# Twelve pairs of down-projection column blocks: the first four k tiles by seven block products (Strassen's algorithm)

## The chip, the cores and the metric

One core of a Trainium2 chip runs the whole kernel. The metric is the device time of one launch in microseconds (us). A TensorE matmul is called here by its moving width: one of 512 columns works on a stationary tile of 128x128 and a moving tile of 128x512.

## The reference, cut to what matters

```python
for layer in range(2):                      # x is (1, 256, 2048) float32
    h = rmsnorm(x, norm_mix_w[layer])
    x = x + mixer(h)                        # retention + RG-LRU, then windowed attention
    h = rmsnorm(x, norm_mlp_w[layer])
    u = relu(h @ w_up[layer])               # w_up   (2048, 8192)
    x = x + (u * u) @ w_down[layer]         # w_down (8192, 2048)
return rmsnorm(x, final_norm_w)
```

## The kernel before

**Blocks and steps.** All projections are cut into 89 blocks. A block is one product of the 256 tokens (two tiles of 128, `TT`) with a weight piece of 2048 rows (16 k tiles of 128) by 512 columns (`NB`), summed in two PSUM banks `acc[:, b % 2, tt]`. It is worked off in a *slot* of 8 *steps* (the code says halves), each of 2 k tiles (a half of one of four loaded *units* of 4 k tiles, 1 MB). float32 precision is had from three products of rounded parts: each operand is a high part and a low part, and a step issues, for 2 k tiles and 2 token tiles, high x high, high x low and low x high, so 12 matmuls of 512 columns (`products`, L1203 to L1218).

**The feeding of a step.** SyncE loads units into the four buffers `raw` (`load`, L488), each as soon as the low part of its last reader has been made. ScalarE rounds a step's 128x1024 weights to `w_hi` (`cut_hi`, L610), then VectorE forms `w_lo = raw - w_hi` (`cut_lo`, L848), and TensorE waits for that (L1207). `w_hi` and `w_lo` are rings of four steps (`RING`). Each engine runs a body once per step k of each slot: first `post(slot, k)`, which is the work on the block before, then the cut for step k + 4 (L811, L1165). The cut for step k + 4 waits until TensorE has used step k (L621). So a cut has three steps of TensorE's time to be finished in.

**The MLP.** An MLP is four chunks of 2048 hidden columns: a chunk is four "up" blocks, `up0` to `up3`, then four "down" blocks of the 2048x2048 piece of `w_down`. The loop of `run_slots` (L210) runs three chunks, a fourth stands behind it, and there are two MLPs.

**Post work of an up block**, in the slot behind it: ScalarE evacuates two token tiles with a ReLU and squares them (`leave`, L649, two times L672 and two times L677); VectorE turns them by 16 transposes of 32x256 (`turn_quadrants`, L1027, 4, 6 and 6 at steps 1, 2, 3); at step 4 ScalarE makes `b_hi` (L630) and VectorE `b_lo` (L862), two instructions each. For `up0` all this is two steps later (`late`, L125), since it is in `WOVEN`: its last two steps are run behind the first two of the block after it, so that a late stationary operand is not waited for. The first down block is woven in the same way.

**Post work of a down block**: VectorE adds its two PSUM banks to the residual `x` (L1070, two instructions of 128x512). TensorE starts block b only when block b - 2 has been evacuated (L1435 to L1440).

What the change touches: the sets and tables of L99 to L106, `late`, `quadrants_at`, `Slot.halves` (L199), the buffers of L284 to L315, `load`, `cut_hi` and `cut_lo`, ScalarE's and VectorE's `post` (L734, L1061), the adds of L1066 to L1070, `products`, and the `body` of each engine.

Of the kernel before, what the change touches and what calls it, by code (L numbers as in the profile page):

```python
# [28 lines left out]
P = 128  # L29
# [3 lines left out]
SEQ = 256  # L33
# [36 lines left out]
def mlp_blocks(last_kind):  # L70
    blocks = []
    for c in range(CHUNKS):
# [81 lines left out]

def quadrants_at(kind, b):

    return QUADRANTS_EARLY if b == ATT_OUT0 else QUADRANTS_AT[kind]


# [30 lines left out]
class Slot:  # L190
# [7 lines left out]

    def halves(self, n):  # L199

        return self.plus(self.b * HALVES + n, PERIOD * HALVES)

    def count(self, table, at, more=0):

# [46 lines left out]
def build(nc, t):  # L251
    ctx = ExitStack()
    with ctx:
# [30 lines left out]
        AREA = 12300  # L284
        area = sb("area", [P, AREA])
        place = {"at": 0}

# [15 lines left out]
        gate_t = take(LG, SEQ)  # L303
        q_t = take(HG, SEQ)
        k_t = take(HG, SEQ)
        v_tok = take(TT, NB)
        o_tok = take(TT, NB)
        p_ret = take(2, DECAY_W)
# [5 lines left out]
        gel = take(SEQ)  # L314
        gel2 = take(SEQ)  # L315
# [15 lines left out]
        den_s = take(TT, GROUP)  # L331
        den_i = take(TT, GROUP)
        final_w = take(D_MODEL)

        acc = ctx.enter_context(nc.psum_tensor("acc", [P, 2, TT, NB], F32))
        bank = ctx.enter_context(nc.psum_tensor("bank", [P, 4, NB], F32))
# [79 lines left out]
        y_act = sem("y_act")  # L416
        y_dve = sem("y_dve")
        stored = sem("stored")


        V_NORM = [0, KT, 2 * KT, 3 * KT]
# [15 lines left out]
        def stationary(b):  # L437

            from_b = (MIX_OUT0 <= b < MLP0 or ATT_OUT0 <= b < MLP1
                      or BLOCKS[b][0] == "down" or (b >= MLP0 and BLOCKS[b][0] in ("res", "fin")))  # L440
            return (b_hi, b_lo) if from_b else (a_hi, a_lo)

        def target(b):

# [11 lines left out]
        def _(sp):  # L456
# [30 lines left out]

            def load(slot, view):  # L488

                for q in range(UNITS):  # L490
                    b, k = piece(slot.b, 2 * q)

                    sp.wait_ge(lo_ready, slot.halves(2 * q + 2 - HALVES))
                    sp.dma_start(raw[:, q], view(row_groups(b)[k // 2], b - slot.b)).then_inc(raw_loaded[q], 16)

            def units(w):

# [111 lines left out]
        def _(act):  # L609
            def cut_hi(slot, n):  # L610

                d, h = divmod(n, HALVES)
                if slot.b * HALVES + n >= NBLK * HALVES:
                    return
                if slot.i is None and slot.b == 0 and d == 0:
                    act.wait_ge((raw_loaded if h % 2 else raw_first)[h // 2], 16)
                elif h % 2 == 0:
                    act.wait_ge(raw_loaded[h // 2], slot.plus(16 * (slot.b + d + 1), 16 * PERIOD))
                if slot.b * HALVES + n >= RING:

                    act.wait_ge(half_used, slot.halves(n - RING + 1))  # L621
                nc.scalar.activation(w_hi[:, h % RING], raw[:, h // 2, 2 * (h % 2):2 * (h % 2) + 2, :],  # L622
                                     ACT.Copy).then_inc(hi_ready, 1)

            def turned_parts(hi, kt, scale, n_turned, n_banks, by_quadrant=False):

# [84 lines left out]
            def attention(g, k):  # L711
# [16 lines left out]
                for tt in range(TT) if k == ATT_AT["out"] else ():  # L728
# [2 lines left out]
                                         bank[:, 2 - 2 * tt, :].rearrange("p (q s) -> p q s", q=PAIRS),  # L731
                                         ACT.Copy).then_inc(att_hi, 1)

            def post(slot, k):  # L734
                b = slot.b - 1
                if b < 0:
                    return
                kind, j = BLOCKS[b]
                if k == late(b) and kind in BY_ACT:
                    leave(slot, kind, j)  # L740
                if k == 1 + late(b) and kind in ("res", "fin"):
                    act.wait_ge(evac_dve, slot.count(N_EVAC_DVE, 0))
                    square_sums(next_norm(b), j)
                if kind in SPLIT and k == out_at(kind, b):
                    hi, _, kt, scale = target(b)
                    for m in range(2):
                        turned_parts(hi, kt + 2 * m, None if scale is None else scale + 2 * m,
                                     slot.count(N_MOVED, -1, INIT_HALVES + m + 1), m, kind in BY_QUADRANT)
                if k == 4 and kind == "res" and j == COLS - 1:
                    root(next_norm(b))  # L750
# [40 lines left out]
                    root(0)  # L791

            def body(slot):
                for k in range(HALVES):
# [44 lines left out]
        def _(dve):  # L839
# [7 lines left out]

            def cut_lo(slot, n):  # L848

                h = n % HALVES  # L850
                if slot.b * HALVES + n >= NBLK * HALVES:
                    return
                dve.wait_ge(hi_ready, slot.halves(n + 1))
                nc.vector.tensor_tensor(w_lo[:, h % RING], raw[:, h // 2, 2 * (h % 2):2 * (h % 2) + 2, :],  # L854
                                        w_hi[:, h % RING].bitcast(F32), ALU.subtract).then_inc(lo_ready, 1)

            def turned_parts(hi, lo, kt, scale, n_split, n_banks, by_quadrant=False):

# [202 lines left out]
            def post(slot, k):  # L1061
# [4 lines left out]
                if k == late(b) and kind in ("res", "down", "fin"):  # L1066
                    dve.wait_ge(half_used, slot.halves(late(b)))
                    for tt in range(TT):
                        xs = x[:, tt, j * NB:(j + 1) * NB]
                        nc.vector.tensor_tensor(xs, xs, acc[:, b % 2, tt, :], ALU.add).then_inc(evac_dve, 1)  # L1070
# [21 lines left out]
                if kind in TURNED and k == out_at(kind, b):  # L1092
                    for m in range(2):
# [4 lines left out]
                        elif kind in PLAIN:  # L1098
                            dve.wait_ge(turned, slot.count(N_MOVED, -1, INIT_HALVES + m + 1))
                            nc.vector.tensor_copy(plain_target(kind, j)(m),  # L1100
                                                  bank[:, m, :].rearrange("p (k s) -> p k s", k=2)
                                                  ).then_inc(turned_out, 1)
                if k == 3 + late(b) and kind == "fin" and j < COLS - 1:
                    weigh(j)
                if k == 3 and kind == "res" and j == COLS - 1:
# [39 lines left out]
                    inverse(0)  # L1145

            def body(slot):
                for k in range(HALVES):
# [53 lines left out]
        def _(pe):  # L1202
            def products(slot, k):  # L1203

                b, h = piece(slot.b, k)
                hi, lo = stationary(b)
                pe.wait_ge(lo_ready, slot.halves(k + 1))  # L1207
                for e in range(2):
                    kt = 4 * row_groups(b)[h // 2] + 2 * (h % 2) + e
                    wh, wl = w_hi[:, k % RING, e, :], w_lo[:, k % RING, e, :]  # L1210
                    first, last = h == 0 and e == 0, h == HALVES - 1 and e == 1
                    for tt in range(TT):
                        xh, xl = (s[:, kt, tt * P:(tt + 1) * P] for s in (hi, lo))
                        a = acc[:, b % 2, tt, :]
                        nc.tensor.matmul(a, xh, wh, start=first, stop=False)  # L1215
                        nc.tensor.matmul(a, xh, wl, start=False, stop=False)  # L1216
                        ins = nc.tensor.matmul(a, xl, wh, start=False, stop=last)  # L1217
                ins.then_inc(half_used, 1)  # L1218

            def turn_x(h):  # L1220
# [212 lines left out]
            def body(slot):  # L1433
# [9 lines left out]
                for k in range(HALVES):  # L1443
# [71 lines left out]
```

## Time and profile before

| | |
|---|---|
| median of three runs | 2006.84 us (2005.88 to 2007.82) |
| span of the profiled execution, first to last instruction | 2005.7 us |
| what lies around the span (median less span) | 1.1 us |
| busy share: TensorE matmul, weight load, VectorE, ScalarE | 100%, 82%, 72%, 51% |
| granted TensorE clock over the span | 1.00 (2.4 GHz) |
| DMA | 382 MB, 191 GB/s |

No device time of the profiled execution itself is given beside its span; the median of the runs stands in for it. The share of TensorE is of modelled durations (a matmul's record overlaps the next one's), so the rate is read from start to start. The other engines' times are averages over stages that differ much; what an edit in the down blocks costs is read from the rows of those slots.

### The profile page before, as it was taken

What the parts mean: (1) busy time and instruction counts of PE and PEld (TensorE: products, weight loads), DVE (VectorE), ACT (ScalarE), POOL (GpSimd) and SP (SyncE); (2) the same over time, 40 slices, a digit from 0 to 9 for tenths busy, and PEclk for the clock granted to TensorE, in tenths of its full rate; (3) what the DMA queues carried; (4) which work ended last, traced back from release to release, by engine and by line L of the source; (5) the groups of instructions that cost most, each with busy time, mean ns of one, the idle gap of its engine ahead of it and who ended that gap; (6) DMA issues with size and microseconds to landing.
All of it is one profiled execution on the core that took longest, in us unless ns stands there. A gap on an engine that the chain in (4) does not pass through costs nothing.

```text
span 2005.7 us, 24710 instructions
## 1 busy us (share of the span) xinstructions
PE 1997.1 (100%) x9161; PEld 1653.1 (82%) x9161; DVE 1450.5 (72%) x2028; ACT 1027.4 (51%) x1360; POOL 45.1 (2%) x55
## 2 busy tenths in 40 slices
PE   9999999999999999999999999999999999999998
PEld 8888888888888888888888878888888888888887
DVE  6777778987558647755889887988548756854875
ACT  6665665455345435434545566555435444534554
POOL 1110110000000000000000000000000000000000
PEclk9999999999999999999999999999999999999999
DMA  8556546556555565555655544565565555565563
GB/s 304 181 176 214 170 167 211 189 189 209 191 189 192 198 195 185 193 195 181 210 189 189 169 162 163 181 203 194 194 197 193 192 190 187 187 209 189 189 201 113
DMA packets 191756, 382.48 MB, mean 191 GB/s; under 512 B 6328, under 2 KB 7616, under 8 KB 191552
## 3 DMA queue, kind: packets, MB, share of 16 engines
q1 hardware_dynamic: 190288, 377.51, 57.0%
q0 software_dynamic: 1216, 3.88, 0.6%
q8 instruction: 48, 0.79, 0.2%
q14 instruction: 28, 0.23, 0.0%
q10 hardware_dynamic: 176, 0.07, 0.0%
HBM read 379.34 MB, written 2.10 MB: 190 GB/s over the span
## 4 chain that ended last, share of the span: by engine, by line
PE 98%; DVE 1%; issue 0%; ACT 0%; DMA 0%; ACTq 0%
PE acc L1215 31%; PE acc L1217 31%; PE acc L1216 31%; DVE area L1052 1%; PE bank L1305 0%; PE bank L1382 0%; PE bank L1406 0%; PE bank L1392 0%; DVE w_lo L854 0%; PE acc L1244 0%; PE acc L1248 0%; PE acc L1252 0%; PE bank L1347 0%; PE bank L1336 0%; PE bank L1337 0%
## 5 line engine op out<-in xcount | busy, mean ns | idle before, releaser
L854 DVE TENSOR_TENSOR w_lo<-raw,w_hi 128x1024 fp32r<-128x1024 f32 x708 | 858.9, 1223 | 497.8 <-ACT w_hi L622 494.9
L622 ACT ACTIVATE w_hi<-raw 128x1024 fp32r<-128x1024 f32 x708 | 743.5, 1060 | 772.3 <-PE acc L1217 771.0
L1215 PE MATMUL acc<-w_hi,a_hi 128*128 128x512 f32 x1552 | 607.1, 391 | 0.0
L1217 PE MATMUL acc<-w_hi,a_lo 128*128 128x512 f32 x1552 | 604.1, 389 | 0.0
L1216 PE MATMUL acc<-w_lo,a_hi 128*128 128x512 f32 x1552 | 604.0, 389 | 0.0
L1215 PE MATMUL acc<-w_hi,b_hi 128*128 128x512 f32 x1264 | 492.3, 389 | 0.0
L1216 PE MATMUL acc<-w_lo,b_hi 128*128 128x512 f32 x1264 | 491.8, 389 | 0.0
L1217 PE MATMUL acc<-w_hi,b_lo 128*128 128x512 f32 x1264 | 491.7, 389 | 0.0
L1215 PEld LDWEIGHTS acc<-w_hi,a_hi 128*128 128x128 f32 x1552 | 291.4, 188 | 61.2 <-issue 0.9
L1217 PEld LDWEIGHTS acc<-w_hi,a_lo 128*128 128x128 f32 x1552 | 291.3, 188 | 60.9
L1216 PEld LDWEIGHTS acc<-w_lo,a_hi 128*128 128x128 f32 x1552 | 291.4, 188 | 60.0
L1215 PEld LDWEIGHTS acc<-w_hi,b_hi 128*128 128x128 f32 x1264 | 237.2, 188 | 49.9 <-issue 0.9
L1217 PEld LDWEIGHTS acc<-w_hi,b_lo 128*128 128x128 f32 x1264 | 237.2, 188 | 49.4
L1216 PEld LDWEIGHTS acc<-w_lo,b_hi 128*128 128x128 f32 x1264 | 237.3, 188 | 49.2
L1052 DVE STREAM_TRANSPOSE turn<-stage 32x256 f32<-32x256 f32 x512 | 223.1, 436 | 7.7
L630 ACT ACTIVATE b_hi<-turn 128x512 fp32r<-128x512 f32 x64 | 37.0, 625 | 107.1 <-DVE turn L1052 107.1
L1052 DVE STREAM_TRANSPOSE turn<-x 32x256 f32<-32x256 f32 x192 | 83.7, 436 | 2.9
L672 ACT ACTIVATE stage<-acc,rinv 128x512 f32<-128x512 f32 x92 | 57.7, 675 | 0.5 <-DVE rinv L887 0.5
L1052 DVE STREAM_TRANSPOSE area<-stage 32x256 f32<-32x256 f32 x112 | 48.8, 436 | 1.6
L1070 DVE TENSOR_TENSOR x<-x,acc 128x512 f32<-128x512 f32 x78 | 49.8, 679 | 0.0
L862 DVE TENSOR_TENSOR b_lo<-turn,b_hi 128x512 fp32r<-128x512 f32 x64 | 41.1, 684 | 0.0
L677 ACT ACTIVATE stage<-stage 128x512 f32<-128x512 f32 x64 | 36.7, 626 | 0.0
(204 smaller groups left out, 602.1 us busy)
## 6 DMA issues: line engine op xcount, KB each, us to landing
raw<-in_mlp_w_up SPq DMA_DIRECT2D x128, 1024.0 KB, 5.3
raw<-in_mlp_w_down SPq DMA_DIRECT2D x128, 1024.0 KB, 5.1
raw<-in_hyb_w_in SPq DMA_DIRECT2D x44, 1024.0 KB, 5.2
raw<-in_attn_w_qkv SPq DMA_DIRECT2D x20, 1024.0 KB, 5.2
raw<-in_hyb_w_out SPq DMA_DIRECT2D x16, 1024.0 KB, 5.1
raw<-in_attn_w_out SPq DMA_DIRECT2D x16, 1024.0 KB, 5.0
raw<-in_hyb_w_in SPq DMA_DIRECT2D x5, 512.0 KB, 9.5
out_y<-x SPq DMA_DIRECT2D x4, 512.0 KB, 3.0
```

Of the source, the lines that this page charges most:

```text
L622: nc.scalar.activation(w_hi[:, h % RING], raw[:, h // 2, 2 * (h % 2):2 * (h % 2) + 2, :], ACT.Copy).then_inc(hi_ready, 1)
L630: nc.scalar.activation(hi[:, kt:kt + 2, :], src, ACT.Copy).then_inc(turned_hi, 1)
L672: ins = nc.scalar.activation(stage[:, tt, :], src, ACT.Relu if kind == "up" else ACT.Copy, scale=s)
L677: nc.scalar.activation(stage[:, tt, :], stage[:, tt, :], ACT.Square).then_inc(squared, 1)
L854: nc.vector.tensor_tensor(w_lo[:, h % RING], raw[:, h // 2, 2 * (h % 2):2 * (h % 2) + 2, :], w_hi[:, h % RING].bitcast(F32), ALU.subtract) ...
L862: nc.vector.tensor_tensor(lo[:, kt:kt + 2, :], src, hi[:, kt:kt + 2, :].bitcast(F32), ALU.subtract).then_inc(turned_out, 1)
L1052: ins = nc.vector.transpose(dst[f * QUAD:(f + 1) * QUAD, :, :, a, :], src[a * QUAD:(a + 1) * QUAD, :, :, f, :])
L1070: nc.vector.tensor_tensor(xs, xs, acc[:, b % 2, tt, :], ALU.add).then_inc(evac_dve, 1)
L1215: nc.tensor.matmul(a, xh, wh, start=first, stop=False)
L1216: nc.tensor.matmul(a, xh, wl, start=False, stop=False)
L1217: ins = nc.tensor.matmul(a, xl, wh, start=False, stop=last)
```

## The change

For 12 pairs of neighbouring down blocks (the four of chunks 0, 1 and 2 in each MLP) the first four k tiles are computed by Strassen's algorithm in Winograd's form: the operands are seen as 2x2 blocks (token tile x k-tile pair, and k-tile pair x column block), and seven products of 6 matmuls take the place of eight. The slot of the pair's first block holds 18 steps, one of them empty, and that of the second holds 2. Steps ("P", p) are the seven products; ("L", h) and ("R", h) are ordinary steps of the left and the right block for h of 2 to 7. The right block is summed in `acc`, the left one in two banks of `bank`.

What is new in a pair: VectorE forms four sums of weights in place in `raw`, 128x1024 each (`add_weights`, behind the cuts of SUM_AFTER), and adds four partial results from PSUM to `x`, 128x512 each (`add_part`, at the step behind P1, P5, P6 and P7). TensorE waits for the first of these before P6, the second before P3, the third before P7. Once in a chunk, behind the turning of `up0`, VectorE forms four token sums of 128x256 (`add_tokens`), ScalarE their high parts and VectorE their low parts, 128x1024 each.

```diff
+QUADRANTS_PAIR = {8: 5, 9: 5, 10: 6}
+PAIR_CHUNKS = CHUNKS - 1
+PAIRS0 = {m + PERIOD * c + COLS + 2 * n for m in (MLP0, MLP1) for c in range(PAIR_CHUNKS) for n in range(2)}
+PAIR_STEPS = [("P", 1), ("L", 2), ("P", 5), ("L", 3), ("P", 6), ("P", 2), ("P", 4), ("P", 7), ("P", 3),
+              ("L", 4), ("L", 5), ("R", 2), ("R", 3), ("R", 4), ("R", 5), ("R", 6), ("R", 7), (None, 0),
+              ("L", 6), ("L", 7)]
+PAIR_SPLIT = 18
+PAIR_FREE = [STEP_OF["P", 4] + 1, STEP_OF["P", 3] + 1, STEP_OF["L", 3] + 1, STEP_OF["L", 5] + 1,
+             STEP_OF["R", 3] + 1, STEP_OF["R", 5] + 1, STEP_OF["R", 7] + 1, STEP_OF["L", 7] + 1]
+SUM_AFTER = {STEP_OF["P", 1]: 5, STEP_OF["P", 5]: 6, STEP_OF["L", 3]: 7, STEP_OF["P", 2]: 4}
+SUM_COUNT = {5: 1, 6: 2, 7: 3, 4: 4}
 WOVEN = ({MIX_OUT0, QKV0, ATT_OUT0}
-         | {m + COLS * n for m in (MLP0, MLP1) for n in range(2 * CHUNKS)})
+         | {m + COLS * n for m in (MLP0, MLP1) for n in range(2 * CHUNKS)}) - PAIRS0
@@ def late(b)
+    if b + 1 in FIRST_PAIRS:
+        return 1
@@ ScalarE, cut_hi
+                elif what is not None and what[0] == "P" and what[1] in SUM_COUNT:
+                    act.wait_ge(weights_added, slot.pairs(4, SUM_COUNT[what[1]], b))
@@ VectorE, cut_lo
+                if b in PAIRS0 and h in SUM_AFTER:
+                    add_weights(slot, b, SUM_AFTER[h])
+            def add_weights(slot, b, p):
+                b11, b21, b12, b22 = (raw[:, q, 2 * e:2 * e + 2, :] for q in range(2) for e in range(2))
+                if p == 5:
+                    ins = nc.vector.tensor_tensor(b11, b12, b11, ALU.subtract)
+                if p == 6:
+                    ins = nc.vector.tensor_tensor(b11, b22, b11, ALU.subtract)
+                if p == 7:
+                    ins = nc.vector.tensor_tensor(b12, b22, b12, ALU.subtract)
+                if p == 4:
+                    ins = nc.vector.tensor_tensor(b21, b21, b11, ALU.subtract)
+                ins.then_inc(weights_added, 1)
+            def add_part(slot, k):
+                for p, tt, cols, src in ((1, 0, left, 1), (5, 1, right, 0), (6, 0, right, 1), (7, 1, left, 1)):
+                    if k == STEP_OF["P", p] + 1:
+                        dve.wait_ge(half_used, slot.halves(k))
+                        nc.vector.tensor_tensor(x[:, tt, cols], x[:, tt, cols], accumulator(slot.b, src),
+                                                ALU.add).then_inc(part_added, 1)
+            def add_tokens(slot):
+                nc.vector.tensor_tensor(s1, a21, a22, ALU.add).then_inc(tokens_added, 1)
+                nc.vector.tensor_tensor(s3, a11, a21, ALU.subtract).then_inc(tokens_added, 1)
+                dve.wait_ge(tokens_added, slot.chunks(4, 1))
+                nc.vector.tensor_tensor(s2, s1, a11, ALU.subtract).then_inc(tokens_added, 1)
+                dve.wait_ge(tokens_added, slot.chunks(4, 3))
+                nc.vector.tensor_tensor(s4, a12, s2, ALU.subtract).then_inc(tokens_added, 1)
@@ VectorE, post
+                if slot.b in PAIRS0:
+                    add_part(slot, k)
+                if b + COLS in FIRST_PAIRS and k == out_at(kind, b):
+                    add_tokens(slot)
+                if b + COLS in FIRST_PAIRS and k == HALVES - 1:
+                    tokens_rest(slot)
@@ TensorE
+            def product(slot, k, p):
+                pe.wait_ge(lo_ready, slot.halves(k + 1))
+                if p in (3, 6, 7):
+                    pe.wait_ge(part_added, slot.pairs(4, {6: 1, 3: 2, 7: 3}[p]))
...
+                for e in range(2):
...
+                    nc.tensor.matmul(a, xh, wh, start=first, stop=False, skip_group_check=True)
+                    nc.tensor.matmul(a, xh, wl, start=False, stop=False, skip_group_check=True)
+                    ins = nc.tensor.matmul(a, xl, wh, start=False, stop=False, skip_group_check=True)
+                ins.then_inc(half_used, 1)
```

Not shown: the counts of steps per slot that the semaphore values follow, the order in which `load` fetches the pair's eight units, a wait before ("R", 6) for `up3`'s turned tokens, and buffers of the mixer that now share space (`v_tok` with `o_tok`, `gel` and `gel2` with `junk`), which make room for the token sums.

## Rows read from the trace of the kernel before

**Rows 1.** The page: span, and busy time by engine.
```profile
span 2005.7 us, 24710 instructions
...
PE 1997.1 (100%) x9161; PEld 1653.1 (82%) x9161; DVE 1450.5 (72%) x2028; ACT 1027.4 (51%) x1360; POOL 45.1 (2%) x55
```

**Rows 2.** The page: the chain that ended last, by engine.
```profile
PE 98%; DVE 1%; issue 0%; ACT 0%; DMA 0%; ACTq 0%
```

**Rows 3.** Timeline, PE: first matmul of the slots behind up1 and up3.
```profile
429.33 0.39 PE L1215 MATMUL acc<-w_hi,a_hi 128*128 128x512 f32 x1
...
472.85 0.39 PE L1215 MATMUL acc<-w_hi,b_hi 128*128 128x512 f32 x1
```

**Rows 4.** Stretches: us, busy of PE, PEld, DVE, ACT, POOL; clock; DMA.
```profile
0.00:5.00 5.00, 3.29 (x14) 2.99 (x15) 0.55 (x2) 1.49 (x2) 0.31 (x5) 1.00 0.55 178
...
463.00:485.00 22.00, 22.00 (x99) 18.22 (x98) 17.96 (x27) 11.74 (x15) 0.00 (x0) 1.00 0.57 195
485.00:507.00 22.00, 22.00 (x99) 18.22 (x98) 15.26 (x20) 9.42 (x10) 0.00 (x0) 1.00 0.61 206
```

**Rows 5.** Groups of instructions, shapes apart: busy us, mean ns of one, idle before.
```profile
L854 DVE TENSOR_TENSOR w_lo<-raw,w_hi 128x1024 fp32r<-128x1024 f32 x708 | 858.9, 1223 | 497.8 <-ACT w_hi L622 494.9
L622 ACT ACTIVATE w_hi<-raw 128x1024 fp32r<-128x1024 f32 x708 | 743.5, 1060 | 772.3 <-PE acc L1217 771.0
...
L1070 DVE TENSOR_TENSOR x<-x,acc 128x512 f32<-128x512 f32 x78 | 49.8, 679 | 0.0
...
L866 DVE SCALAR_TENSOR_TENSOR a_lo<-turn,vecs,a_hi 128x256 fp32r<-128x256 f32 x48 | 20.0, 478 | 0.0
...
L1023 DVE TENSOR_TENSOR area<-area 128x1024 f32<-128x1024 f32 x8 | 9.8, 1224 | 0.3
```

**Rows 6.** Timeline, DVE: start, us, idle before; the slots of up2, up3, downs.
```profile
430.66 2.35 DVE L854 TENSOR_TENSOR w_lo<-raw,w_hi 128x1024 fp32r<-128x1024 f32 x2
434.53 1.23 DVE L854 TENSOR_TENSOR w_lo<-raw,w_hi 128x1024 fp32r<-128x1024 f32 x1 [1.53 <-ACT w_hi L622]
...
445.39 1.22 DVE L854 TENSOR_TENSOR w_lo<-raw,w_hi 128x1024 fp32r<-128x1024 f32 x1
...
468.74 2.35 DVE L854 TENSOR_TENSOR w_lo<-raw,w_hi 128x1024 fp32r<-128x1024 f32 x2
471.43 1.23 DVE L854 TENSOR_TENSOR w_lo<-raw,w_hi 128x1024 fp32r<-128x1024 f32 x1 [0.34 <-ACT w_hi L622]
474.14 1.23 DVE L854 TENSOR_TENSOR w_lo<-raw,w_hi 128x1024 fp32r<-128x1024 f32 x1 [1.49 <-ACT w_hi L622]
...
502.49 1.27 DVE L1070 TENSOR_TENSOR x<-x,acc 128x512 f32<-128x512 f32 x2
```

**Rows 7.** Timeline, ACT: the same stretches.
```profile
429.37 1.99 ACT L622 ACTIVATE w_hi<-raw 128x1024 fp32r<-128x1024 f32 x2
431.27 1.25 ACT L672 ACTIVATE stage<-acc,rinv 128x512 f32<-128x512 f32 x2
...
433.45 1.05 ACT L622 ACTIVATE w_hi<-raw 128x1024 fp32r<-128x1024 f32 x1
...
473.05 1.06 ACT L622 ACTIVATE w_hi<-raw 128x1024 fp32r<-128x1024 f32 x1 [1.66 <-PE acc L1217]
...
476.20 1.06 ACT L622 ACTIVATE w_hi<-raw 128x1024 fp32r<-128x1024 f32 x1
```

**Rows 8.** Timeline, all engines: TensorE released by a late VectorE result.
```profile
1136.31 0.48 DVE L995 MEMSET bank<- 64x512 f32 x1
...
1136.85 0.48 PEld L1382 LDWEIGHTS bank<-area 64*64 64x64 f32 x21 [0.58 <-DVE bank L995]
```

**Rows 9.** Timeline, PE: first two matmuls behind a break in the stream.
```profile
25.45 0.48 PE L1215 MATMUL acc<-w_hi,a_hi 128*128 128x512 f32 x1
...
25.76 0.40 PE L1216 MATMUL acc<-w_lo,a_hi 128*128 128x512 f32 x1
```

**Rows 10.** DMA issues: count, KB each, median us from issue to landing.
```profile
raw<-in_mlp_w_down SPq DMA_DIRECT2D x128, 1024.0 KB, 5.1
```

More of the change, by code:

```diff
@@ new lines, with ring, step_at, pair_step @@
+NSTEP = [PAIR_SPLIT if b in PAIRS0 else len(PAIR_STEPS) - PAIR_SPLIT if b in PAIRS1 else HALVES
+         for b in range(NBLK)]
+STEP0 = [sum(NSTEP[:b]) for b in range(NBLK + 1)]
+def ring(b, k):
+    return (STEP0[b] + k) % RING
+def step_at(b, n):
+    while b < NBLK and n >= NSTEP[b]:
+        n -= NSTEP[b]
+        b += 1
+    return b, n
+def pair_step(b, k):
+    if b in PAIRS0:
+        return PAIR_STEPS[k]
+    if b in PAIRS1:
+        return PAIR_STEPS[PAIR_SPLIT + k]
+    return None
@@ L107, with weight_at @@
+def weight_at(b, k):
+    what = pair_step(b, k)
+    if what is None:
+        return k // 2, k % 2, b + 1
+    side, h = what
+    first = b if b in PAIRS0 else b - 1
+    if side == "P":
+        q, e = PIECE_OF[h]
+        return q, e, first + 1
+    n = PAIR_UNITS.index((side, h // 2))
+    return n % UNITS, h % 2, first + 1 + n // UNITS
 WOVEN_ORDER = ([(0, k) for k in range(6)] + [(1, 0), (1, 1), (0, 6), (0, 7)]
@@ L199, in halves, with pairs, chunks @@
     def halves(self, n):
-        return self.plus(self.b * HALVES + n, PERIOD * HALVES)
+        per = STEP0[self.b + PERIOD] - STEP0[self.b] if self.i is not None else 0
+        return self.plus(STEP0[self.b] + n, per)
+    def pairs(self, per, n, b=None):
+        return self.plus(per * sum(p < (self.b if b is None else b) for p in PAIRS0) + n, 2 * per)
+    def chunks(self, per, n):
+        return self.plus(per * sum(p + 1 < self.b for p in FIRST_PAIRS) + n, per)
     def count(self, table, at, more=0):
@@ L732, in attention, with tokens @@
                                          ACT.Copy).then_inc(att_hi, 1)
+            def tokens(slot):
+                act.wait_ge(tokens_added, slot.chunks(4, 4))
+                nc.scalar.activation(s_hi[:, :, :, :], s_sum[:, :, :, :], ACT.Copy).then_inc(tokens_hi, 1)
             def post(slot, k):
@@ L793, in body @@
             def body(slot):
-                for k in range(HALVES):
+                for k in range(NSTEP[slot.b]):
                     post(slot, k)
@@ L848, in cut_lo @@
             def cut_lo(slot, n):
-                h = n % HALVES
-                if slot.b * HALVES + n >= NBLK * HALVES:
+                b, h = step_at(slot.b, n)
+                if b >= NBLK:
                     return
+                what = pair_step(b, h)
+                if what == (None, 0):
+                    return
+                q, e, _ = weight_at(b, h)
                 dve.wait_ge(hi_ready, slot.halves(n + 1))
-                nc.vector.tensor_tensor(w_lo[:, h % RING], raw[:, h // 2, 2 * (h % 2):2 * (h % 2) + 2, :],
-                                        w_hi[:, h % RING].bitcast(F32), ALU.subtract).then_inc(lo_ready, 1)
+                nc.vector.tensor_tensor(w_lo[:, ring(b, h)], raw[:, q, 2 * e:2 * e + 2, :],
+                                        w_hi[:, ring(b, h)].bitcast(F32),
+                                        ALU.subtract).then_inc(lo_ready, 2 if what == ("R", HALVES - 1) else 1)
@@ new lines, in add_part @@
+            def add_part(slot, k):
+                left, right = (slice((BLOCKS[slot.b + d][1]) * NB, (BLOCKS[slot.b + d][1] + 1) * NB) for d in (0, 1))
+                for p, tt, cols, src in ((1, 0, left, 1), (5, 1, right, 0), (6, 0, right, 1), (7, 1, left, 1)):
[3 more added lines that the diff above has]
+                                                ALU.add).then_inc(part_added, 1)
@@ L857, in turned_parts, with tokens_rest @@
+            def tokens_rest(slot):
+                dve.wait_ge(tokens_hi, slot.chunks(1, 1))
+                nc.vector.tensor_tensor(s_lo[:, :, :, :], s_sum[:, :, :, :], s_hi[:, :, :, :].bitcast(F32),
+                                        ALU.subtract).then_inc(tokens_lo, 1)
             def turned_parts(hi, lo, kt, scale, n_split, n_banks, by_quadrant=False):
@@ L1068, in post @@
                     for tt in range(TT):
-                        xs = x[:, tt, j * NB:(j + 1) * NB]
-                        nc.vector.tensor_tensor(xs, xs, acc[:, b % 2, tt, :], ALU.add).then_inc(evac_dve, 1)
+                        c = BLOCKS[b + (b in PAIRS0) - (b in PAIRS1)][1]
+                        xs = x[:, tt, c * NB:(c + 1) * NB]
+                        nc.vector.tensor_tensor(xs, xs, accumulator(b, tt), ALU.add).then_inc(evac_dve, 1)
                 if k == 1 + late(b):
@@ L1147, in body @@
             def body(slot):
-                for k in range(HALVES):
+                for k in range(NSTEP[slot.b]):
                     post(slot, k)
@@ L1203, in products @@
             def products(slot, k):
-                b, h = piece(slot.b, k)
+                what = pair_step(slot.b, k)
+                if what is None:
+                    b, h = piece(slot.b, k)
+                    begins = h == 0
+                else:
+                    side, h = what
+                    b = slot.b + (side == "L") - (slot.b in PAIRS1)
+                    begins = what == PAIR_STEPS[1]
+                joins = what is not None
                 hi, lo = stationary(b)
@@ L1209, in products @@
                     kt = 4 * row_groups(b)[h // 2] + 2 * (h % 2) + e
-                    wh, wl = w_hi[:, k % RING, e, :], w_lo[:, k % RING, e, :]
-                    first, last = h == 0 and e == 0, h == HALVES - 1 and e == 1
+                    wh, wl = w_hi[:, ring(slot.b, k), e, :], w_lo[:, ring(slot.b, k), e, :]
+                    first, last = begins and e == 0, h == HALVES - 1 and e == 1
                     for tt in range(TT):
                         xh, xl = (s[:, kt, tt * P:(tt + 1) * P] for s in (hi, lo))
[L1214 to L1217, printed above, removed]
+                        a = accumulator(b, tt)
+                        nc.tensor.matmul(a, xh, wh, start=first, stop=False, skip_group_check=joins)
+                        nc.tensor.matmul(a, xh, wl, start=False, stop=False, skip_group_check=joins)
+                        ins = nc.tensor.matmul(a, xl, wh, start=False, stop=last, skip_group_check=joins)
@@ new lines, in products @@
+                ins.then_inc(half_used, 2 if what == ("R", HALVES - 1) else 1)
+            def product(slot, k, p):
+                b = slot.b
+                pe.wait_ge(lo_ready, slot.halves(k + 1))
+                if p == 5 and b in FIRST_PAIRS:
+                    pe.wait_ge(tokens_lo, slot.chunks(1, 1))
+                if p in (3, 6, 7):
+                    pe.wait_ge(part_added, slot.pairs(4, {6: 1, 3: 2, 7: 3}[p]))
+                a = accumulator(b, 1 if p in (1, 6, 7) else 0)
+                if p in (2, 4):
+                    a = accumulator(b + 1, p // 2 - 1)
+                for e in range(2):
+                    wh, wl = w_hi[:, ring(b, k), e, :], w_lo[:, ring(b, k), e, :]
+                    if p in (1, 2, 4):
+                        kt, tt = {1: (e, 0), 2: (2 + e, 0), 4: (2 + e, 1)}[p]
+                        xh, xl = (s[:, kt, tt * P:(tt + 1) * P] for s in (b_hi, b_lo))
+                    else:
+                        xh, xl = (s[:, {5: 0, 6: 1, 7: 2, 3: 3}[p], e, :] for s in (s_hi, s_lo))
+                    first = p in (1, 5) and e == 0
+                    nc.tensor.matmul(a, xh, wh, start=first, stop=False, skip_group_check=True)
+                    nc.tensor.matmul(a, xh, wl, start=False, stop=False, skip_group_check=True)
+                    ins = nc.tensor.matmul(a, xl, wh, start=False, stop=False, skip_group_check=True)
@@ L1442, in body @@
                     pe.wait_ge(turned_out, slot.count(N_TURNED, -1, INIT_HALVES))
-                for k in range(HALVES):
+                for k in range(NSTEP[b]):
+                    what = pair_step(b, k)
+                    if what == (None, 0):
+                        continue
+                    if what is not None and what[0] == "P":
+                        product(slot, k, what[1])
+                        continue
+                    if b in FIRST_PAIRS and k == LAST_TURNED_AT:
+                        pe.wait_ge(turned_out, slot.count(N_TURNED, 0, INIT_HALVES))
+                    if what == ("R", 2):
+                        pe.wait_ge(part_added, slot.pairs(4, 4))
                     if b == 0 and k >= PIECED:
```

76 lines of the change are left out of this document (60 added, 16 removed).

## The prediction
> **What bounds the kernel now.** I read the page first: the span is 2005.7 us and TensorE is busy for all of it, VectorE for 72%, ScalarE for 51% [rows 1]. The chain that ended last is 98% TensorE [rows 2]. So TensorE's stream of matmuls is the bound, and what the others do is free while they stay ahead of it. The pace: two slots of 96 matmuls lie between the two starts in [rows 3], 43.52 us, which is 0.2267 us for a matmul, 2.72 for a step of 12 and 1.36 for a product of 6. The clock is 1.00 throughout [rows 4], so nothing is to be won there.
>
> The share of 72% hides where VectorE is near its limit. Over the post work of up blocks it is busy 17.96 of 22 us, in the stretch behind, mostly down steps, 15.26 [rows 4]. Each step needs one cut by ScalarE (1.06 us) and one by VectorE (1.22) [rows 5], in that order, and a cut may begin only when the step four before has been used. From that step's end it is 0.20 to ScalarE's start and 1.09 more to VectorE's [rows 3, 7, 6] (472.85, 473.05, 474.14), so a cut is ready 2.5 us behind, with 8.16 allowed: VectorE can run 5.6 us late before TensorE feels it. In the seven products the same three steps last only 4.08, and the reserve falls to 1.5.
>
> **What it removes.** One product of 6 matmuls in each of 12 pairs: 72 x 0.2267 = 16.3 us, all on the path, if TensorE never waits.
>
> **What it adds, by pair.** Seven cuts serve the first k tiles instead of four: three more on ScalarE (1.06) and VectorE (1.22). Four weight sums on VectorE: fp32 tensor_tensor of 128x1024 from SBUF, for which the attention's own row has 1.224 us [rows 5]. Four part adds of 0.68 [rows 5]. That is 3.7 + 4.9 + 2.7 = 11.3 us more VectorE work in 40 us of TensorE's, which the average could hold. But it is crowded: all of it belongs to the first 15 us of a pair or shortly before. So I walk the queue in the program's order. Back to back, VectorE's instructions follow each other faster than they last: a cut after 1.12 (two in 2.35), a part add after 0.59 (two in 1.27) [rows 6]; I take 1.14 for a cut and a weight sum, 0.60 for an add, and full durations where another engine waits. A TensorE step held by VectorE starts some 0.14 behind: 0.06 to the release (1136.79 to 1136.85 [rows 8]) and 0.08 for the longer first interval (0.31 for 0.23 [rows 9]).
>
> **Second pair of a chunk.** Time 0 is the start of ("L", 6) of the pair before, which frees the ring for the cut of P1. VectorE's starts: P1 1.30, sum for P5 2.44, L2 3.58, two evacuations of the right block 4.72 (end 5.99), P5 5.91, sum for P6 7.05, L3 8.19, sum for P7 9.33, two evacuations of the left block 10.47, P6 11.67, add of P1 12.81 (end 13.50), P2 13.41, sum for P4 14.55 (end 15.78). Now ScalarE must round that sum, 15.82 to 16.88, before VectorE can go on: P4 16.92 (end 18.15), add of P5 18.06, P7 18.66, P3 19.80, add of P6 20.94, end 21.63. TensorE: P1 may not overwrite `acc` before the evacuation, so it starts at 6.13 instead of 5.44 (0.69 late); L2, P5, L3, P6, P2 follow without a gap to 17.02; P4 waits for its low part until 18.29 (1.27); P7 waits for the add of P6, since it accumulates on what that add reads, from 19.65 to 21.77 (2.12). Sum 4.1 us.
>
> The add of P6 decides because it stands in VectorE's queue behind the cuts of P7 and P3, which are ahead of their use. Thirteen cuts and sums, seven adds and evacuations are 19.0 us, from 1.30 on; P7 is due at 17.7. Even without the 1.2 us in which VectorE waits for ScalarE, it would be 2.8 late. Behind it only cuts at ordinary pace follow, and the queue recovers.
>
> **First pair.** Time 0 is its start, like 472.85 in [rows 3]. VectorE's cut of P1 starts at -4.11 (468.74 [rows 6], late because of up2's turning), then sum -2.97, L2 -1.83, P5 -0.60, sum 0.54, L3 1.68, sum 2.82, P6 3.96, add of P1 5.10. ScalarE rounds P6 at 1.81 and then evacuates and squares up3, so the cut of P2 starts 3.15 later (473.05 to 476.20 [rows 7]), 4.96; VectorE has it at 6.06, sum 7.20, ScalarE P4 8.47, VectorE P4 9.57 (end 10.80), add of P5 10.71, P7 11.31, P3 12.45, add of P6 13.59, end 14.28. TensorE wants P4 at 10.88 and gets it at 10.94, wants P7 at 12.30 and gets it at 14.42. Sum 2.2 us. Up3's turning comes five to seven steps later, at steps of 2.72, and by the same walk its `b_lo` is done 1.1 us before ("R", 6) asks: nothing.
>
> **Token sums, once a chunk.** They stand behind up0's `b_lo`, before the cut that starts at 430.66 [rows 6]. Four adds of 128x256: the nearest row is 0.478 us [rows 5]; with two waits on own results some 1.7. Then ScalarE's part (1.06) and VectorE's (1.14). ScalarE's evacuation of up1 (431.27 [rows 7]) waits in its queue behind these: the token part starts at 432.47, the cut behind it at 433.44, the evacuation at 434.41, 3.1 us later than before. Up1's turning and the cuts between move with it: the cut that started at 445.39 [rows 6] starts at 448.5 and ends at 449.8, while its step is due at 429.33 + 7 x 2.72 = 448.4 [rows 3]. Stall 1.5 us. If the adds took 0.2 each it would be under 0.6; if ScalarE's gap were filled, nothing. At up3's slot the queue has caught up.
>
> **Costed at nothing.** The loads: a unit lands 5.1 us after its issue [rows 10]. The tightest is the first right unit, issued when P4's low part is made (18.15), landed at 23.3, when ScalarE's queue comes to it (P7 is used at 23.1); its step is due 8.2 us after P7's start. If it came 3 us late it would still be hidden. The lost weaving: the down steps that need up3 now come at step 15. The shared mixer buffers: no wait is added and their readers are in order; bounded by 0 and 1 us.
>
> **Sum.** Per chunk 1.5 + 2.2 + 4.1 = 7.8 us, six chunks 47.0; less 16.3 is +30.7 on a span of 2005.7, so 2036.4, and with the 1.1 us between span and median of the runs **2037.5 us**.
>
> [...]
>
> **The rivals.**
> 1. *VectorE stalls TensorE as walked* (2024 to 2056): 0.78. Low end: no stall at the token sums (-9) and the waits of VectorE on ScalarE half as long (-5). High end: 0.1 us more for each cut and sum between unlike instructions, 13 in either walk and some 6 in the token stretch, +19.
> 2. *VectorE keeps up* (faster). What speaks for it: the stretch over down blocks has 6.7 us idle of 22 [rows 4]. It needs the add of P6 to end within 17.7 us of ("L", 6), so its queue from 1.30 on must shrink from 20.3 to 16.2, which weight sums of some 0.2 us instead of 1.14 would do in the second pair. Then 16.3 are won: 1990.5. Against it, the sum has the same shape, type and operation as the row of 1.224. 0.07. If stalls just eat the gain (2.7 us a chunk), about 2007: 0.05.
> 3. *More than walked*: the first right unit and those queued behind it land late, or sums in place cost more than between two buffers. Five us more a chunk is 2067: 0.06.
> 4. *The clock falls.* In the first 5 us TensorE was busy for 3.29 and the granted clock was 1.00 [rows 4]; in the walk it is busy for about as much of the 5 us around a stall of 2.1. Were the steps from P1 to P3 of each pair, 15 us, at 1.2 GHz, 12 x 15 = 180 more would give about 2217: 0.04. The Trainium skill ("TensorE: Matmul & The Clock Gate", section "HAM oscillation") warns that gaps in the matmul stream throw TensorE back to 1.2 GHz; the row shows no fall at such a share.
>
> **How the numbers follow.** 0.2% (4 us) is about what a measurement of this kernel can tell from no change. Faster 0.07, same 0.05, slower 0.88. The range 2024 to 2056 is case 1's own and leaves out the others.
>
> **What would show it.** In the profile after: TensorE's busy share below 100%, with waits of TensorE for the part add and for `w_lo` of some 40 us together; 72 matmuls fewer; chunks with P7 about 2.1 us late in either pair, P4 1.3 late in the second pair only, P1 0.7 late in the second only; one stall of 1.5 us near the end of up1's post work; VectorE without idle from the second pair's P1 cut to P6's add, but for about 1.2 us. Wrong would be: no waits of TensorE (case 2), waits for DMA (case 3), a granted clock under 1.00 (case 4), or a weight sum that is not 1.2 us.

## The result, and the profile after

The changed kernel takes 2048.21 us (median of four runs, 2044.73 to 2050.33) against 2007.07 us (four runs; the 2006.84 given before are three of them): the ratio is 1.0206, with a 95% interval of 1.0192 to 1.0221. It is slower by 41 us, where 30.7 were forecast; 2048.2 lies inside the range of 2024 to 2056.

The page of the changed kernel, its span, busy shares and the chain that ended last (compare [rows 1, 2]):

```profile
span 2048.5 us, 25055 instructions
...
PE 2004.6 (98%) x9089; PEld 1644.6 (80%) x9089; DVE 1584.1 (77%) x2190; ACT 1067.0 (52%) x1402; POOL 45.2 (2%) x55
...
PE 71%; DVE 16%; issue 8%; ACT 5%; ACTq 0%; DMA 0%; DVEq 0%
```

The profiled execution of the changed kernel is the slowest of its four (2050.33 us). The 72 matmuls are gone (9161 to 9089). The chain, 98% TensorE before, now runs through VectorE for 16% and ScalarE for 5%, though VectorE's share of the span rose only from 72 to 77%. The share says little; the chain says who is late.

The weight loads' waits (engine, line waited for: us in total, times, longest) say where. L1420 is the first matmul of a product, L1000 the part add, L974 the low part of a cut:

```profile
PEld acc L1420 <- DVE x L1000: 26.9, 12, 2.2
PEld acc L1394 <- DVE w_lo L974: 9.9, 14, 1.4
PEld bank L1420 <- DVE w_lo L974: 8.5, 12, 1.2
PEld acc L1420 <- issue: 5.6, 6, 0.9
```

In the order of the rows: P7, held in every pair for the part add of P6; the step in the slot of up1's post work, twice in each of six chunks (two short waits of 0.3 together lie elsewhere); P4, where the longest are the six of the second pairs (the first pairs have 0.23 each); P1 of the second pairs. The last row names no releaser; the matmul's own row names the evacuation, L1235:

```profile
PE acc L1420 <- DVE x L1235: 3.1, 6, 0.5
```

Together the four rows are 50.9 us, where the prediction named some 40. Behind each wait the first interval between matmuls is some 0.1 longer, and the ordinary gap between weight loads (about 0.04) is contained in the rows.

One second pair in VectorE's timeline (start, us, idle before). The walk's time 0 lies at 513.5:

```profile
520.53 1.22 DVE L987 TENSOR_TENSOR raw<-raw 128x1024 f32<-128x1024 f32 x1
521.67 1.22 DVE L974 TENSOR_TENSOR w_lo<-raw,w_hi 128x1024 fp32r<-128x1024 f32 x1
...
528.00 1.22 DVE L991 TENSOR_TENSOR raw<-raw 128x1024 f32<-128x1024 f32 x1
530.43 1.23 DVE L974 TENSOR_TENSOR w_lo<-raw,w_hi 128x1024 fp32r<-128x1024 f32 x1 [1.21 <-ACT w_hi L731]
531.57 0.68 DVE L1000 TENSOR_TENSOR x<-x,acc 128x512 f32<-128x512 f32 x1
532.17 2.35 DVE L974 TENSOR_TENSOR w_lo<-raw,w_hi 128x1024 fp32r<-128x1024 f32 x2
534.44 0.68 DVE L1000 TENSOR_TENSOR x<-x,acc 128x512 f32<-128x512 f32 x1
```

The sum for P6 was walked at 7.05 and stands at 7.0; the add of P6 was walked at 20.94 and stands at 20.9. The sum for P4 ends at 529.2, ScalarE rounds it, VectorE idles 1.21 us, then come the cut of P4, the add of P5, the cuts of P7 and P3, and only then the add for which TensorE waits. TensorE's timeline of the same pair:

```profile
530.57 0.39 PE L1422 MATMUL bank<-w_hi,b_lo 128*128 128x512 f32 x1
531.71 0.50 PE L1420 MATMUL bank<-w_hi,b_hi 128*128 128x512 f32 x1 [0.75 <-DVE w_lo L974]
532.04 0.39 PE L1421 MATMUL bank<-w_lo,b_hi 128*128 128x512 f32 x1
...
532.97 0.40 PE L1422 MATMUL bank<-w_hi,b_lo 128*128 128x512 f32 x1
535.17 0.50 PE L1420 MATMUL acc<-w_hi,s_hi 128*128 128x512 f32 x1 [1.81 <-DVE x L1000]
535.52 0.40 PE L1421 MATMUL acc<-w_lo,s_hi 128*128 128x512 f32 x1
...
536.87 0.63 PE L1420 MATMUL acc<-w_hi,s_hi 128*128 128x512 f32 x1
537.30 0.63 PE L1421 MATMUL acc<-w_lo,s_hi 128*128 128x512 f32 x1
```

P4 comes 1.14 behind its predecessor instead of 0.23, P7 2.20. The last two rows show what was not in the sum of the forecast: from 536.4 on, eight matmuls follow each other at 0.43 instead of 0.23. Two stretches of the same pair, and the one around P7 of the first pair that had a fall too (us, busy of PE, PEld, DVE, ACT, POOL; clock; DMA):

```profile
531.10:536.20 5.10, 2.68 (x10) 1.91 (x11) 5.10 (x7) 3.20 (x4) 0.00 (x0) 1.00 0.59 204
536.50:539.50 3.00, 3.00 (x9) 2.33 (x8) 2.19 (x3) 1.06 (x1) 0.00 (x0) 0.50 1.00 375
...
1421.82:1426.92 5.10, 3.28 (x14) 2.22 (x13) 5.10 (x7) 3.20 (x4) 0.00 (x0) 1.00 0.60 204
```

In the second pair TensorE was busy for 2.68 of 5.10 us, and right behind it the granted clock is 0.50, the level of 1.2 GHz. The stretch lasts 3.41 us and costs 1.7. The trace has seven of them while TensorE has work, in all six second pairs and one first pair, always beginning 1.2 to 1.4 us behind P7's late start.

**The account.** One weight sum as the chain of waits has it in two chunks that follow each other (start us, us, what):

```profile
652.29 1.23 DVE raw L985
...
833.21 1.23 DVE raw L985
```

With one such stretch in between, that is 180.9 us for a chunk, where eight slots of 21.76 were 174.1 [rows 3]. Of the 6.8 more, 1.7 are the clock. The other 5.1 are 7.85 of lost time less 2.7 for the removed matmuls. The intervals between matmuls show what the 7.85 are made of: about 7.3 at the places where TensorE was held, and the rest intervals that are slightly longer than 0.2267 without a wait. Over six chunks and seven stretches: 6 x 5.1 + 7 x 1.7 = 42.7, and the spans differ by 42.8.

### The profile page after: what moved, and what is told of

The parts are those of the page before. It is cut to its first block, busy times and chain, and to the rows that moved or that the text cites. A ratio compares the mean times of both kernels' runs of the same rounds, so it can differ in the third digit from the quotient of the medians.

```text
span 2048.5 us, 25055 instructions
## 1 busy us (share of the span) xinstructions
PE 2004.6 (98%) x9089; PEld 1644.6 (80%) x9089; DVE 1584.1 (77%) x2190; ACT 1067.0 (52%) x1402; POOL 45.2 (2%) x55
## 4 chain that ended last, share of the span: by engine, by line
PE 71%; DVE 16%; issue 8%; ACT 5%; ACTq 0%; DMA 0%; DVEq 0%
PE acc L1394 20%; PE acc L1395 20%; PE acc L1396 20%; DVE w_lo L974 5%; DVE turn L1216 5%; ACT w_hi L731 3%; PE bank L1394 2%; PE bank L1395 2%; PE bank L1396 2%; DVE x L1000 1%; ACT stage L781 1%; PE acc L1420 1%; PE acc L1422 1%; DVE raw L987 1%; DVE raw L985 1%
## 5 line engine op out<-in xcount | busy, mean ns | idle before, releaser
L974 DVE TENSOR_TENSOR w_lo<-raw,w_hi 128x1024 fp32r<-128x1024 f32 x744 | 901.0, 1223 | 406.6 <-ACT w_hi L731 403.3
L1394 PE MATMUL acc<-w_hi,b_hi 128*128 128x512 f32 x784 | 305.6, 390 | 0.0
L1395 PE MATMUL acc<-w_lo,b_hi 128*128 128x512 f32 x784 | 305.1, 389 | 0.0
L1396 PE MATMUL acc<-w_hi,b_lo 128*128 128x512 f32 x784 | 305.0, 389 | 0.0
L1394 PEld LDWEIGHTS acc<-w_hi,b_hi 128*128 128x128 f32 x784 | 147.2, 188 | 31.5 <-issue 0.9
L1396 PEld LDWEIGHTS acc<-w_hi,b_lo 128*128 128x128 f32 x784 | 147.2, 188 | 30.7
L1395 PEld LDWEIGHTS acc<-w_lo,b_hi 128*128 128x128 f32 x784 | 147.2, 188 | 30.2
L1394 PE MATMUL bank<-w_hi,b_hi 128*128 128x512 f32 x288 | 113.7, 395 | 0.0
L1395 PE MATMUL bank<-w_lo,b_hi 128*128 128x512 f32 x288 | 112.5, 391 | 0.0
L1396 PE MATMUL bank<-w_hi,b_lo 128*128 128x512 f32 x288 | 112.3, 390 | 0.0
L1394 PEld LDWEIGHTS bank<-w_hi,b_hi 128*128 128x128 f32 x288 | 55.0, 191 | 12.1
```

Of the source, the lines that this page charges most:

```text
L974: nc.vector.tensor_tensor(w_lo[:, ring(b, h)], raw[:, q, 2 * e:2 * e + 2, :], w_hi[:, ring(b, h)].bitcast(F32), ALU.subtract).then_inc(lo_ ...
L1394: nc.tensor.matmul(a, xh, wh, start=first, stop=False, skip_group_check=joins)
L1395: nc.tensor.matmul(a, xh, wl, start=False, stop=False, skip_group_check=joins)
L1396: ins = nc.tensor.matmul(a, xl, wh, start=False, stop=last, skip_group_check=joins)
```

## The experiments

All times are medians beside runs of the kernel before on the same chip, whose median was 2005.7 to 2005.9 us there. The changed kernel was not run again beside them; its 2048.21 stands beside 2007.07, so a difference taken from it is uncertain by some 1 us.

**p6_early.** One add moved by one place.

```diff
-                    if k == STEP_OF["P", p] + 1:
-                        dve.wait_ge(half_used, slot.halves(k))
+                    if k == STEP_OF["P", p] + (p != 6):
+                        dve.wait_ge(half_used, slot.halves(STEP_OF["P", p] + 1))
```

> VectorE's part add of P6 is moved one place up its queue, ahead of the weight cut of P3. Theory 1 (VectorE's queue holds TensorE): the add ends 1.14 us earlier in either pair, so each of the 12 waits before P7 falls from about 2.1 to 1.0 us and the time falls by 13.7 us, from 2048.2 to 2034.5; should the clock then no longer fall to 1.2 GHz, by the 12 us of the seven falls as well, to 2022.5. Theory 2 (the products themselves or their PSUM traffic are slow, and the waits only mark the place): nothing that VectorE does in another order helps, 2048 within 4.

Measured: 2024.12 us, ratio 1.0092 (1.0075 to 1.0109), and the clock was not at 0.50 in either MLP. The waits of P7:

```profile
PEld acc L1420 <- DVE x L1000: 13.3, 12, 1.1
PEld acc L1394 <- DVE w_lo L974: 9.8, 14, 1.4
PEld bank L1420 <- DVE w_lo L974: 8.5, 12, 1.2
```

26.9 became 13.3: 13.6 us less, where the walk says 13.7, and the other rows stand still. The remaining 10.5 of the 24.1 us won are put down to the clock: the seven stretches, 11.9 us in the trace of the changed kernel, are gone. So the place of one instruction of 0.68 us in VectorE's queue was worth 24 us of 2048. Theory 2 falls.

**tokens_later.** The parts of the token sums in up2's slot.

```diff
-                if b + COLS in FIRST_PAIRS and k == HALVES - 1:
+                if b + COLS - 1 in FIRST_PAIRS and k == HALVES - 2:
                     tokens(slot)
...
+                if b + COLS - 1 in FIRST_PAIRS and k == 0:
+                    dve.wait_ge(tokens_added, slot.chunks(4, 4))
-                if b + COLS in FIRST_PAIRS and k == HALVES - 1:
+                if b + COLS - 1 in FIRST_PAIRS and k == HALVES - 2:
                     tokens_rest(slot)
```

> The high and low parts of the token sums are made in up2's slot instead of up1's; the four adds stay. Theory 1: ScalarE's evacuation of up1 moves back by only 1.7 us instead of 3.1, the cut that missed its step by 1.4 now ends on time, and the stalls of 0.2 and 1.4 us in that slot go: 8 to 9 us less, about 2039.5. The clock falls, which all stand in the pairs, stay. Theory 2 (the stall there is of the adds alone): under 2 us, 2047.

Measured: 2044.72 us (2041.35 to 2048.3), 3.5 less than the changed kernel and not the 8.7 expected. In the trace the stall is gone whole: of the 9.9 us in which a step waited for `w_lo` in `acc` the two short ones elsewhere, 0.3 in all, are left, the other two are unchanged (26.9 and 8.5), and the profiled execution, with eight stretches of half clock, has a span of 2039.6, which is 8.9 less, or 10.6 at equal clock. Some 9 of the 10.6 lie in the six chunks, 1.5 in each (from P7 of one first pair to the next, 181.1 us with two stretches where the changed kernel has 180.9 with one). The mean granted clock of the four runs was 0.989 to 0.992, where those of the changed kernel had 0.993 to 0.995: more stretches at half clock, in a number that differs from run to run, ate the rest of the gain. By an estimate from these means, at 1.7 us a stretch and with the end of the span, at half clock in both, taken off, the changed kernel had 5 to 7 and this one 8 to 12. The mechanism is as walked; the expectation that the clock's falls would stay the same was wrong.

**no_sums.** `SUM_AFTER` and `SUM_COUNT` empty.

> The four sums of weights are left out (the products then read the plain weights, so this part of the computation is wrong), and ScalarE's waits for them; cuts, part adds and token sums stay. Theory 1: VectorE's queue is 4.6 us shorter and never waits for ScalarE in it; by the same walk only 0.55 us before each P7 is left of 6.2 us per chunk, the clock no longer falls, and with the token stall (1.4) the time is about 2005.7 - 16.3 + 6 x 2.5 + 2 + 1.5 = 2008. Theory 2 (part adds and the extra cuts alone are too much, or the products are slow): above 2030.

Measured: 2006.96 us (2006.52 to 2008.24 in ten runs), ratio 1.0005 (0.9995 to 1.0014), no fall of the clock.

```profile
PEld acc L1394 <- DVE w_lo L974: 10.5, 16, 1.4
PEld acc L1420 <- DVE x L1000: 8.1, 12, 0.7
```

P7 still comes late in each pair: it starts 0.64 behind its predecessor instead of 0.23, and the next interval is 0.1 longer, 0.5 in all where the walk has 0.55. P4 and P1 are on time. So the four sums, with ScalarE's waits for them, 12 x 4 x 1.22 = 59 us of VectorE's work, cost 41 us of the kernel's time, the clock's 12 among them; what is left just eats the removed matmuls. Theory 1 holds.

**evac_early.** The evacuation ahead of the cut of L2.

```diff
+                if slot.b in PAIRS0 and k == PAIR_SPLIT - 1:
+                    dve.wait_ge(half_used, slot.halves(PAIR_SPLIT))
+                    for tt in range(TT):
...
+                        nc.vector.tensor_tensor(xs, xs, accumulator(slot.b, tt), ALU.add).then_inc(evac_dve, 1)
-                if k == late(b) and kind in ("res", "down", "fin"):
+                if k == late(b) and kind in ("res", "down", "fin") and b not in PAIRS0:
```

> VectorE evacuates the right block one place earlier, ahead of the cut of L2. Theory 1: P1 of the second pair is no longer held (0.7 us), but VectorE's queue is as long as before, so P4 waits 1.9 instead of 1.3 and P7 the same 2.1: time unchanged, 2048 within 2 (or the clock's falls vary by one or two, 1.7 us each). Theory 2 (each wait is a cost of its own): 6 x 0.7 = 4 us less, 2044.

Measured: 2048.63 us against 2048.21.

```profile
PEld acc L1426 <- DVE x L1000: 26.9, 12, 2.2
PEld bank L1426 <- DVE w_lo L974: 13.4, 12, 2.0
PEld acc L1400 <- DVE w_lo L974: 9.7, 14, 1.4
```

P1's wait is gone, P4's grew from 8.5 to 13.4. The time is unchanged, as theory 1 has it. Here a wait taken away in front of a full queue came back at the next place: the length of VectorE's queue up to the add of P6 decides, not the single waits.

**three_edits.** p6_early, tokens_later and evac_early together, order of the steps unchanged.

> The order of the steps as in the changed kernel, with P6's add ahead of the cut of P3, the token parts in up2's slot and the right block's evacuation ahead of the cut of L2. Theory 1: 3.75 us of waiting per chunk by the walk (P4 1.9 and P7 1.0 in the second pair, P7 0.8 in the first), 2005.7 - 16.3 + 22.5 + 2.5 = 2014.4, so that spreading the products is worth the other 20 us. Theory 2 (moving the adds only moves the waits): 2020 or more.

Measured: 2016.74 us, ratio 1.0054 (1.0038 to 1.0069); no fall of the clock, though P4 of the second pair came 1.97 us behind its predecessor and P7 1.06. That is 2.3 more than theory 1 has, and below the 2020 of theory 2.

**spread_only.** A third ordinary step of the left block, L4, is put between the products (L2 and L3 stood there already), P7 is moved ahead of P4, and the loads follow the order in which buffers come free. Not shown: the table of the buffers' release (`PAIR_FREE`) that follows from it, and one step more of waiting for the first two units of an MLP.

```diff
-PAIR_STEPS = [("P", 1), ("L", 2), ("P", 5), ("L", 3), ("P", 6), ("P", 2), ("P", 4), ("P", 7), ("P", 3),
-              ("L", 4), ("L", 5), ("R", 2), ("R", 3), ("R", 4), ("R", 5), ("R", 6), ("R", 7), (None, 0),
+PAIR_STEPS = [("P", 1), ("L", 2), ("P", 5), ("L", 3), ("P", 6), ("L", 4), ("P", 2), ("P", 7), ("P", 4), ("P", 3), ("L", 5),
+              ("R", 2), ("R", 3), ("R", 4), ("R", 5), ("R", 6), ("R", 7), (None, 0),
-PAIR_UNITS = [("L", 0), ("R", 0), ("L", 1), ("L", 2), ("R", 1), ("R", 2), ("R", 3), ("L", 3)]
+PAIR_UNITS = [("L", 0), ("R", 0), ("L", 1), ("L", 2), ("R", 2), ("R", 3), ("R", 1), ("L", 3)]
...
-                for q in range(UNITS):
+                for q in (2, 0, 1, 3) if b0 in PAIRS1 else range(UNITS):
```

> Only the order of the steps and of the loads is changed; P6's add, the token parts and the evacuation stay as in the changed kernel. Theory 1: by the walk 0.7 us before P1 and 0.8 before P7 of the second pair are left, with the 1.4 us of the token sums 2.9 per chunk, no clock falls: 2005.7 - 16.3 + 17.4 + 2.5 = 2009.3. Theory 2: as the changed kernel less the clock's 12 us, 2036.

Measured: 2018.34 us, ratio 1.0060 (1.0045 to 1.0076), no fall of the clock. 30 us less than the changed kernel, but 9 more than expected. TensorE's and ScalarE's timelines at P1 of a second pair show where most of the 9 lie:

```profile
514.57 0.39 PE L1398 MATMUL bank<-w_hi,b_lo 128*128 128x512 f32 x1
516.57 0.49 PE L1422 MATMUL acc<-w_hi,b_hi 128*128 128x512 f32 x1 [1.61 <-DVE x L1237]
```

```profile
512.93 3.13 ACT L733 ACTIVATE w_hi<-raw 128x1024 fp32r<-128x1024 f32 x3 [2.31 <-DMA raw<-in_mlp_w_down]
```

The new places of the units let a load of the next pair start later, ScalarE waited 2.31 us for it, and VectorE's queue and the evacuation behind it moved along: P1 came 2.00 behind its predecessor instead of 0.90 (1.88 to 2.04 in the six chunks), some 6.4 us in all. The walk had no loads in it. P7 of the second pair came only 0.59 behind its predecessor, so less was lost there than walked; the rest of the 9 was not traced.

**all_four.** spread_only and three_edits together.

> The seven products are spread among ordinary steps (P1 L2 P5 L3 P6 L4 P2 P7 P4 P3 L5, with the loads in the order that their buffers come free), P6's part add stands ahead of the next cut, the token parts are made in up2's slot, and the right block is evacuated ahead of the cut of L2. Theory 1: VectorE's work per pair is the same to an instruction, but it is due over five more microseconds; the walk leaves 0.35 us of waiting per chunk, no clock falls, and the 72 matmuls are won but for some 2.5 us of longer intervals in the products: 2005.7 - 16.3 + 2.1 + 2.5 = 1994. Theory 2 (VectorE is simply too full in the chunk, 11 us more work per pair): waits turn up elsewhere, at the ordinary steps, and the time stays above 2010.

Measured: 1997.07 us, ratio 0.9954 (0.9940 to 0.9967). Faster than the kernel before, by 0.46%. The walk had 1994, 3 us less; theory 2 falls. The page has TensorE's share at 100% again:

```profile
span 1993.5 us, 25061 instructions
...
PE 1984.2 (100%) x9089; PEld 1636.3 (82%) x9089; DVE 1582.6 (79%) x2190; ACT 1068.3 (54%) x1402; POOL 45.1 (2%) x55
```

Of the weight loads' waits for a part add this is left:

```profile
PEld acc L1430 <- DVE x L1002: 2.5, 7, 0.6
```

VectorE's work is what it was in the changed kernel (1584.1 us there); its due times and its order differ. Neither half was enough alone: spread_only has 2018.34 and three_edits 2016.74.

**all_four_again.** The same kernel, run beside the one below.

> The same kernel as all_four, beside loads_first on the same chip: 1997 within 1.5 by either theory.

Measured: 1997.23 us, ratio 0.9953 (0.9940 to 0.9967).

**loads_first.** all_four, with the early free buffer also loaded first in a second pair.

```diff
-                for q in (2, 0, 1, 3) if b0 in PAIRS1 else range(UNITS):
+                for q in (2, 0, 1, 3) if b0 in PAIRS1 or b0 - 1 in PAIRS1 and b0 in PAIRS0 else range(UNITS):
```

> As all_four, but for a second pair the left block's second unit, whose buffer comes free first, is also issued first. In all_four ScalarE's cut for P1 and L2 of the second pair waited for that load (it landed 7.8 us after its issue), 0.3 us before P1 in VectorE's queue, and TensorE lost 0.8 us per chunk. Theory 1: the wait for DMA goes, P1 and P6 of the second pair start on time or 0.3 earlier, and 1 to 3 us are won: about 1995 where all_four has 1997. Theory 2 (the 0.8 us are VectorE's own queue): no difference.

Measured: 1995.09 us (1994.69 to 1996.0), ratio 0.9945 (0.9931 to 0.9958), beside all_four at 1997.23 (1995.49 to 1997.46). ScalarE's waits for the down weights fell from 36.9 us (20 times, all_four) and 33.1 (18 times, all_four_again) to 19.1 (12 times):

```profile
ACT w_hi L733 <- DMA raw<-in_mlp_w_down: 19.1, 12, 2.4
```

This is the best kernel of the study, 0.55% under the one before. The profiled executions of both have practically the same span (1993.8 and 1993.5), so of the 2 us only the medians speak, and the intervals of the two ratios overlap: that TensorE gains by it is not shown. ScalarE's waits for the weight sum of P5 (L987) grew at the same time from 10.5 to 19.9 us.

## Why the prediction was right, and where it was off

- *The matmuls removed*: 72, as counted. In the trace of the changed kernel the intervals inside the second pair's crowded stretch are 0.2311 us on average (46 intervals from 519.94 to 530.57) where 0.2267 was taken; in no_sums the same 46 intervals are 0.2302, so it is not the weight sums that make them longer. Over the chunks with pairs such intervals add up to some 3.7 us, not in the forecast, and not traced further.
- *Second pair, 4.1 us*: P1 0.67, P4 0.91, P7 1.97 late by the intervals (0.90, 1.14, 2.20 less 0.23), with 0.10 to 0.12 more behind each, 3.9 in all. P4 was walked 1.27 and took 1.0; TensorE had itself lost 0.2 by the longer intervals before it.
- *First pair, 2.2 us*: P4 0.1 and P7 2.1, as walked. "Up3's turning: nothing" held.
- *Token sums, 1.5 us*: 1.3 by the intervals, 1.5 by what tokens_later won in a chunk, by way of ScalarE's evacuation as walked; tokens_later took it away.
- *VectorE decides by its queue up to the add of P6*: shown by p6_early (13.6 us of waiting gone for one place in the queue) and evac_early (nothing won).
- *A weight sum of 1.22 us*: 1.219 to 1.222 in four groups of 12, and the next instruction 1.13 to 1.14 behind it (520.53 to 521.67 above), as taken in the walk.
- *What failed* is the step "the clock falls", put as a rival at 0.04 and at nothing in the sum. The argument was that at 3.29 us busy of 5 the clock had stayed at 1.00 [rows 4] and that a stall of 2.1 leaves about as much. Around P7 of the second pair the busy time was 2.68 of 5.10, lower than that row, since P4's and P7's stalls lie 3.5 us apart and add up; but first pairs had a fall too, one in this trace, at 3.28 of 5.10, and four in that of tokens_later. So a row from the first microseconds was no bound for a gap of 2.2 us in the stream. The price was off as well: not 15 us a pair, but one stretch of 3.41 us at half clock, 1.7 us, in seven of twelve pairs: 11.9 us. With that the forecast of +30.7 on the span becomes +42.6, and 42.8 was measured. The rest of the sum, 7.8 us per chunk, came out at 7.85. That closeness is in part luck: the waits themselves are 0.5 shorter than walked, and the slightly longer intervals, which the sum did not have, make up for it. The term was mis-sized, at 0 instead of 12; the mechanism that was forecast carried the other 31.
- *The other rivals*: VectorE all but kept up only where the sums were left out, or the products spread and the queues reordered (2007 and 1997). Loads did not hold TensorE in the changed kernel, though ScalarE waited 12.9 us for down weights (51.4 in p6_early, where TensorE's other waits stood still); they did once the products were spread.

## What to carry to other kernels

Saved matmuls count only if the engines that feed TensorE can prepare the replacement in the time it is due, so walk their queues in program order at the crowded place; shares over the span (72 to 77% here) show nothing of it. When a wait names an instruction, look at what stands ahead of that instruction on its engine: moving one add of 0.68 us past one cut won 24 us, and spreading the short products, together with three changes of the order in the queues, turned a loss of 41 us into a gain of 9. Price a stall with what it does to the clock as well: here gaps of 2.2 us between two matmuls cost up to 1.7 us beyond their length, and gaps of 2.04 and less did not.

## What the runs showed of the hardware that was not expected

Every stretch at 1.2 GHz in the MLPs came behind a gap in which two matmuls started 2.20 to 2.22 us apart, and none came in the profiled executions whose gaps were 1.97 and then 1.06 (three_edits), 1.15 and 1.07 (p6_early) or 1.88 to 2.04 alone (spread_only). Of the twelve gaps of 2.20 in the changed kernel seven were followed by one: all six that had P4's stall 3.5 us ahead and one of six that had not. In tokens_later it was four of six and four of six. In evac_early, where P4's stall was longer (1.97), it was all six and two of six. So P4's stall alone does not decide; of 36 gaps of this length 23 were followed by a fall. The runs of tokens_later differ by 7 us (2041.35 to 2048.3), which is four stretches of 1.7. The Trainium skill ("TensorE: Matmul & The Clock Gate", section "HAM oscillation") says that gaps in the stream bring TensorE back to 1.2 GHz; the traces agree for 23 of the 36 gaps of 2.20 us, though that section speaks of longer ones than any in these MLPs, and they show no fall for the shorter ones. What exactly decides was not tried.
